# Sparse attention of the prompt: one sequence of heads across blocks, y transposes and output halves moved

## What is computed

```
for each block i of 128 queries, t = 128*i .. 128*i + 127:
    sc  = sum over 8 index heads of relu(iq . ik) * iw          (keys up to t)
    idx = top 256 of sc
    p   = softmax(q . k / 8 over idx), 8 heads, 2 key heads     y_dsa = p . v
out = concat(y_gla, y_dsa) @ w_out                              (1024 x 1024)
h   = layer_norm(alpha * x + out)
```

## Time and profile before

| | us |
|---|---|
| median of three executions | 3746.54 |
| lowest, highest | 3743.01, 3746.85 |
| the profiled execution, its time | 3748.45 |
| its span | 3746.8 |
| its mean granted clock of TensorE | 0.905 |

### The profile page before, as it was taken

One profiled execution on the slowest core, in us unless ns is written; L12 is line 12 of the kernel. 1 busy time (PEld: TensorE's weight loads), 2 busy tenths in 40 slices (PEclk: granted clock), 3 DMA queues, 4 the chain that ended last, 5 costly groups with the idle time before them and its releaser, 6 DMA issues. The chain is left out here.

```text
span 3746.8 us, 53513 instructions
## 1 busy us (share of the span) xinstructions
PE 3308.3 (88%) x20539; PEld 2829.9 (76%) x20539; DVE 1605.0 (43%) x2853; ACT 1089.8 (29%) x2145; POOL 340.2 (9%) x440
## 2 busy tenths in 40 slices
PE   8998884665798997999999997987997999999997
PEld 7797763343444555999999997983665999999997
DVE  2186661993676523111113564432454111113566
ACT  2223541323333233111113443212443111112443
POOL 1100102122111000000000002340000000000002
PEclk9998885786688778999999998996998999999999
DMA  4211014223000001111112111222001111112111
GB/s 130 57 35 30 24 35 118 68 67 127 29 17 17 14 15 40 45 45 45 45 39 98 39 49 48 49 69 86 32 25 43 45 45 41 43 45 94 40 56 49
DMA packets 238053, 190.85 MB, mean 51 GB/s; under 512 B 53762, under 2 KB 215956, under 8 KB 237844
## 3 DMA queue, kind: packets, MB, share of 16 engines
q1 hardware_dynamic: 230148, 170.73, 15.1%
q0 software_dynamic: 7728, 17.71, 1.5%
HBM read 158.73 MB, written 31.38 MB: 51 GB/s over the span
## 5 line engine op out<-in xcount | busy, mean ns | idle before, releaser
L1980 PE MATMUL ffn1u_ps<-h_hi,ffn1u_whi 128*128 128x384 f32 (+1 forms) x1056 | 348.0, 330 | 9.5 <-DVE h_lo L2042 9.5
L1980 PE MATMUL ffn0u_ps<-h_hi,ffn0u_whi 128*128 128x384 f32 (+1 forms) x1056 | 344.8, 327 | 8.8 <-DVE h_lo L2042 8.8
L1980 PE MATMUL ffn1u_ps<-h_lo,ffn1u_whi 128*128 128x384 f32 (+1 forms) x1056 | 347.9, 329 | 0.0
L1980 PE MATMUL ffn1u_ps<-h_hi,ffn1u_wlo 128*128 128x384 f32 (+1 forms) x1056 | 347.8, 329 | 0.0
L1980 PE MATMUL ffn0u_ps<-h_hi,ffn0u_wlo 128*128 128x384 f32 (+1 forms) x1056 | 344.9, 327 | 0.0
L1980 PE MATMUL ffn0u_ps<-h_lo,ffn0u_whi 128*128 128x384 f32 (+1 forms) x1056 | 344.8, 326 | 0.0
L197 PE MATMUL ine_ps<-ine_w_hi,ine_x_hi 128*128 128x256 f32 (+2 forms) x864 | 265.4, 307 | 5.1 <-DVE ine_w_lo L213 5.0
L197 PE MATMUL ine_ps<-ine_w_hi,ine_x_lo 128*128 128x256 f32 (+2 forms) x864 | 250.6, 290 | 0.0
L197 PE MATMUL ine_ps<-ine_w_lo,ine_x_hi 128*128 128x256 f32 (+2 forms) x864 | 250.2, 290 | 0.0
L1980 PEld LDWEIGHTS ffn1u_ps<-h_hi,ffn1u_whi 128*128 128x128 f32 x1056 | 198.9, 188 | 9.9 <-DVE ffn1u_wlo L2024 9.9
L1980 PEld LDWEIGHTS ffn0u_ps<-h_hi,ffn0u_whi 128*128 128x128 f32 x1056 | 198.7, 188 | 9.2 <-DVE ffn0u_wlo L2024 9.2
(11 more groups left out here) (464 smaller groups left out, 7344.7 us busy)
## 6 DMA issues: line engine op xcount, KB each, us to landing
ffn0u_raw<-in_ffn_w_gu_dram SPq DMA_DIRECT2D x44, 512.0 KB, 3.8
ffn1u_raw<-in_ffn_w_gu_dram SPq DMA_DIRECT2D x44, 512.0 KB, 3.8
ffn0d_w<-in_ffn_w_down_dram SPq DMA_DIRECT2D x88, 128.0 KB, 2.2
ffn1d_w<-in_ffn_w_down_dram SPq DMA_DIRECT2D x88, 128.0 KB, 2.2
smp_Kp<-in_cache_k_dram SPq DMA_DIRECT2D x128, 64.0 KB, 1.9
smp_Vp<-in_cache_v_dram POOLq DMA_DIRECT2D x96, 64.0 KB, 2.2
ine_w<-in_w_in_even_dram SPq DMA_DIRECT2D x5, 1024.0 KB
scratch_h<-ine_stage SPq DMA_DIRECT2D x20, 256.0 KB, 2.5
```

The source lines that it names most:

```text
L1980: last = nc.tensor.matmul(ps[:, t, k2, 0:n], wp[:, k2, k, :], hp[:, k, t0:t0 + n], start=(k == 0 and j == 0), stop=(k == KD - 1 and j == 2))
```

## The change

Four things are done, all in `dsa_out`:

1. The heads of all places form one sequence. Scores, row maximum and exponential of head 0 of place i + 1 are issued at the spot where those of a ninth head of place i would be: scores ahead of the transposes of head 7, the row maximum between the early and late rounds of head 7, the exponential after head 7's copies, ahead of `deviation`.
2. The y transposes of place i, with ACT's copies, move from the end of place i to place i + 1, behind the values of head 0 on PE and behind the exponential of head 1 and `scale` on ACT. `scale` of places 1 and later moves with them. The list of slots follows. The last place's stay at the end.
3. The query transposes of the next place come first in the list of passes, and the list no longer holds the output halves. The dots move up in it.
4. The output halves are added to the shares of heads 1 and 2 (the second and third head) behind what these hold already.

```diff
-        out = [("out", s, 0), ("out", s, 1)]
+        out, more = [("out", s, 0), ("out", s, 1)], []
         if s == 0:
-            out += [("iq", S0 + 1)] + dots(BLOCK[S0 + 1], range(2))
+            more = [("iq", S0 + 1)] + dots(BLOCK[S0 + 1], range(2))
...
-        if s + 1 < NT:
-            out.append(("q", s + 1))
-        return out
+        q = [("q", s + 1)] if s + 1 < NT else []
+        return q + more, out
...
-        u, r = passes(s), rounds(s)
+        (u, out), r = passes(s), rounds(s)
...
-        return [(u[n * per:(n + 1) * per], r[n * rper:(n + 1) * rper]) for n in range(NH)]
+        return [(u[n * per:(n + 1) * per] + out[n - 1:n][:n], r[n * rper:(n + 1) * rper]) for n in range(NH)]
...
+            if n == 0 and i >= 1:
+                slots += [("y", i - 1, 0), ("y", i - 1, 1)]
...
+                scores(0, 0)
                 for i in range(NT):
-                    T, share = tile(i), shares(i)
-                    scores(i, 0)
+                    share = shares(i)
                     for n in range(NH):
                         if n + 1 < NH:
                             scores(i, n + 1)
+                        elif i + 1 < NT:
+                            scores(i + 1, 0)
                         transpose_probs(i, n)
...
                         values(i, n)
-                    pe.wait_ge(y_done, i + 1)
-                    for hf in range(2):
...
+                        if n == 0 and i >= 1:
+                            y_transposes(i - 1)
+                y_transposes(NT - 1)
...
                         if n + 1 < NH:
                             exps(i, n + 1)
+                        elif i + 1 < NT:
+                            exps(i + 1, 0)
+                        if n == 0 and i >= 1:
+                            if i >= 2:
+                                scale(i - 1)
+                            copy_y(i - 1)
                     deviation(i)
...
                         if n + 1 < NH:
                             row_max(i, n + 1)
+                        elif i + 1 < NT:
+                            row_max(i + 1, 0)
```

More of the change, by code:

```diff
@@ L1032, in passes @@
             return [("index_keys", 0), ("index_keys", 1), ("iq", S0), ("keys", 0), ("keys", 1), ("q", 0)] + dots(BLOCK[S0], range(4))
[L1033 removed]
+        out, more = [("out", s, 0), ("out", s, 1)], []
         if s == 0:
[L1035 removed]
+            more = [("iq", S0 + 1)] + dots(BLOCK[S0 + 1], range(2))
         elif s == 1:
[L1037 removed]
+            more = dots(BLOCK[S0 + 1], range(2, 4))
         elif s + S0 < NT:
[L1039 to L1042 removed]
+            more = [("iq", s + S0)] + dots(BLOCK[s + S0], range(4))
+        q = [("q", s + 1)] if s + 1 < NT else []
+        return q + more, out
     def rounds(s):
@@ L1303, in _, with y_transposes @@
                         bank7(u)
+                def y_transposes(i):
+                    T = tile(i)
+                    pe.wait_ge(y_done, i + 1)
+                    for hf in range(2):
+                        slot_free(("y", i, hf))
+                        for k in range(4):
+                            c0 = (T_GR, T_DQ)[hf] + k * P
+                            last = nc.tensor.transpose(bank(("y", i, hf))[:, k * P:(k + 1) * P], T[:, c0:c0 + P], st.ident[:, :])
+                        last.then_inc(t_done, 1)
+                scores(0, 0)
                 for i in range(NT):
-                    T, share = tile(i), shares(i)
-                    scores(i, 0)
+                    share = shares(i)
                     for n in range(NH):
@@ L1403, in _, with copy_y @@
                     bank7(u)
+                def copy_y(i):
+                    for hf in range(2):
+                        act.wait_ge(t_done, number[("y", i, hf)] + 1)
+                        if hf == 0 and i >= 2:
+                            act.wait_ge(p7_done, pass_no[("out", i - 1, 1)] + 1)
+                        nc.scalar.copy(YT[:, i % 2, 4 * hf:4 * hf + 4, :],
+                                       bank(("y", i, hf)).rearrange("p (a t) -> p a t", a=4)).then_inc(t_read, 1)
+                exps(0, 0)
                 for i in range(NT):
                     share = shares(i)
-                    exps(i, 0)
                     for n in range(NH):
@@ L1414, in _ @@
                             exps(i, n + 1)
-                    deviation(i)
[L1416 to L1422, removed]
+                        elif i + 1 < NT:
[4 more added lines that the diff above has]
+                            copy_y(i - 1)
+                    deviation(i)
+                    if i == 0:
+                        scale(0)
+                copy_y(NT - 1)
+                scale(NT - 1)
                 copy_x(NT - 1)
```

17 lines of the change are left out of this document (7 added, 10 removed).

## The result

The changed kernel takes 3694.8 us (median of 4 executions, 3690.7 to 3714.8) against 3744.8 for the kernel before in the same comparison: a ratio of 0.9878, interval 0.9841 to 0.9914. A second comparison gave 0.9856, 0.9839 to 0.9872. The forecast was 3737, its range 3716 to 3753. One execution of the experiments, 6541.7 us at a granted clock of 0.57, was disturbed and is left out everywhere.

What follows compares the result with a forecast made beforehand. VectorE and what holds it up bound places 0 to 4, TensorE places 5 to 7. Terms -22.6 + 16.9 - 1.0 - 3.1 + 0.6 = -9.2 us took the median 3746.54 to 3737; range 3716 to 3753.

Steps and rivals of the forecast that it cites:

- (a): Boundaries into places 1 to 4: early head 0 removes VectorE's four first-row-maximum waits, 22.6 us gained at best.
- (b): Late y transposes remove TensorE's wait for the scaled output; three such waits go in places 5 to 7, 3.1 us.
- (c): Output halves at heads 1 and 2: VectorE's waits for them in places 0 to 4 go from 59.3 to 76.2, losing 16.9.
- the full-clock walk: Step-by-step count of place 2 with TensorE at full clock: VectorE waits 9.8 us for the halves, 11.7 before.
- rival 1: Half-clock stretches at three boundaries vanish with the idle time: about 28 us gained, 3718 us; chance 0.13.
- (d): Earlier dots and query transposes: shared-bank copy waits cost 0; small score waits inside heads of places 0 to 4 lose 1 us.
- (e): ScalarE's table switches stay two per boundary; waits for y's copy in places 6 and 7 cost 0.6 us, bounds 0 and 4.
- (f): SP's H ring reload and POOL's shift start later but are wanted later still: no effect, bound 1 us.
- Rival 3: Long products come a head later, the clock returning only during half 0: slower, 3762 us, or 3750 in milder form; chance 0.17.
- Rival 2: VectorE's longer waits for the halves use up the boundary gain: 3742 to 3750 us, 3746; chance 0.20.

Runs made afterwards that it cites:

- the kernel before with its fills: Kernel before plus useless products in the y waits ending places 0 to 3 and at heads 5, 6, 7 of every place: 3737.7 us.
- the one filled in places 0 to 4: Changed kernel plus six useless products ahead of the transposes of heads 5, 6 and 7 in places 0 to 4 only: 3690.2 us.
- changed kernel filled: Changed kernel plus six useless products ahead of the transposes of heads 5, 6 and 7 in every place: 3695.1 us.
- the filled boundary: Kernel before, order unchanged, plus 20 useless products in TensorE's wait for y at the ends of places 0 to 3: 3729.8 us.

## Why the prediction was wrong, step by step

**(a) Row maxima at the boundaries, -22.6: right.** All four waits are gone, though 4.35 us came back as waits of head 2 in places 2 and 4. The 22.6 also hold a part that is the old trace's half clock: in the kernel before with its fills the same four waits are 16.0. What I put down to the early head is won mostly by the late y, as the run without the early head shows.

**(b) The y wait, -3.1 in places 5 to 7: right.** One wait of 0.9 us is left, at the very end. TensorE's whole idle time there fell by less, from 14.6 to 13.3 us. Lengths times clock went from 128.6 to 125.9, 2.7 us. This measure is coarse: the changed kernel and the one filled in places 0 to 4 run the same instructions there and give 125.9 and 120.2. Counting time at half clock instead (67 to 26 us, worth half of 41) leaves 24.4 - 20.5 = 3.9 us to the order. All that these counts carry is that the order's own gain there is a few microseconds, as forecast.

**(c) The halves, +16.9: wrong, and the first of the two steps that failed.** The prediction said: "I take 16.9, because the earlier trace rows is the state in which each of these heads begins." The halves of places 2 and 3 in the changed kernel:

```profile
1036.39 0.69 DVE L1508 SCALAR_TENSOR_TENSOR dsa_X<-dsa_X,dsa_ps 128x512 f32<-128x512 f32 x1 [5.62 <-PE dsa_ps L1224]
...
1051.18 0.69 DVE L1508 SCALAR_TENSOR_TENSOR dsa_X<-dsa_X,dsa_ps 128x512 f32<-128x512 f32 x1 [5.59 <-PE dsa_ps L1224]
...
1116.30 0.69 DVE L1508 SCALAR_TENSOR_TENSOR dsa_X<-dsa_X,dsa_ps 128x512 f32<-128x512 f32 x1 [2.92 <-PE dsa_ps L1224]
...
1130.27 0.69 DVE L1508 SCALAR_TENSOR_TENSOR dsa_X<-dsa_X,dsa_ps 128x512 f32<-128x512 f32 x1 [5.94 <-PE dsa_ps L1224]
```

Place 2 waits 11.2 us where I took 16.7 and the full-clock walk gave 9.8; place 3 waits 8.9 where I took 19.0. All ten add up to 56.4, not 76.2, below the 60 at which the prediction called itself wrong (its other sign, a stage that changes by more than 25 us, was met too: 55.3). The term was mis-sized by 19.8 us: 3.8 in place 0, 5.5 in place 2, 10.1 in place 3, and 1 or less either way in the other two.

What failed is the extra that I put on for half clock. With the clock up (0.94, changed kernel filled) the ten waits add up to 51.1 us, and the walk at full clock had put them 8 below the 59.3, at 51.3. In place 3 I carried the half clock of the old trace into a schedule in which it isn't there: it is back at 1099.1, 0.6 us into the place and 17 before the first half is added. In place 2 the half clock was there as assumed, until 1024.0, 12.8 us into the place, but it cost less. The walk has half 0 end 25.7 us after the first row maximum at full clock and 7 later at half. It ended 28.7 us after it, so 3.0 later, and VectorE wanted it at 23.2, not 22.7. The clock at half through the first 10 us of place 0 cost less than assumed as well; that place I haven't taken apart.

**The clock in places 5 to 7: no term at all, the second failure.** The sum had 3.1 and 0.6 us of order there. The measured 24.4 us are mostly clock: 0.79 to 0.91, worth 20 to 22 by the two counts above. The runs don't show what raised it. The prediction's own view of the windows showed place 5 TensorE-bound at 0.73, so a change of clock acts on their full length, and it was priced nowhere, neither in the sum nor in rival 1, which counted only VectorE's waits in places 0 to 4. This is what put the result 21 us below the range's end.

**(d) 1 us of small score waits: mis-sized.** They went from 10.0 to 5.2 us, and 4.35 of the 5.2 are the new waits of head 2. The wait for the shared bank's copy is 2.0 us in three, in time that VectorE doesn't miss, as said.

**(e) Table switches: right where they were priced.** Head 1's transposes wait for y's copy 0.8 us in one in the late places, for which I had 0.6, and 2.7 us in two in places 0 to 4, where I had none; there TensorE doesn't set the time. The load starts 0.02 us after the read of the accumulator ends (1094.76, 1094.78), and the square root at 1096.08, again 0.02 us after the load: no drain, so the further 4 us that the Trainium skill (ScalarE: Activation LUTs, What ACT_TABLE_LOAD costs) would add didn't come in this order either.

**(f) SP and POOL: nothing**, as said.

**The rivals.** Rival 1 is the nearest, but only part of it took place. Its figure for places 0 to 4 (22.6 + 8 + 1 = 31.6) stands beside 30.7 measured, though its parts came out otherwise (halves 2.9, small waits 4.8). Of its three stretches one shrank and two grew, and the stage's mean clock is 0.85, where it asked for 0.90. I gave it 0.13 because a stretch began ahead of the wait and because short heads lose the clock by themselves. Both are true and neither answers the question, which is when the clock comes back. With a 4.59 us wait in the middle the stretch into place 3 lasted 23.8 us with TensorE busy 78% of it; with none and 95% busy it lasted 10.2. The Trainium skill (TensorE: Matmul & The Clock Gate, HAM oscillation) says that a wait between bursts that throttles the array makes each next burst start slow; the filled boundary agrees as far as it goes (0.50 to 1.00 behind it, 18.9 us), though the stretch that is gone had begun ahead of the wait. And a wait is not all of it: the changed kernel keeps about 152 us at half clock without a wait for y at the boundaries, and the 61 us piece with the halves together is 94% busy. Rival 3 had the clock come back with the long products of half 0; in places 2 and 3 of the changed kernel it came back 5 and 10 us before they began (at 1029.1 and 1109.0). Rival 2's own sum, 4 to 8 us above the forecast, gives 3741 to 3745, not the 3742 to 3750 it states. Rivals 2 and 3 are the time that the kernels with one part missing take (3747, 3759), not that of the whole.

**What stays open.** Why the clock comes back after 10 us at one boundary and 27 at another is not settled: 9.67 of 10.20 us busy in one, 26.27 of 27.20 in the other. Nor is why the executions of one kernel fall into groups 20 us apart (the early head without the late y: 3722, 3729, 3747, 3770), nor what sets the clock of places 5 to 7, some 20 us of the 50: the early head there is worth 9.4 us of it, the fills far ahead, in places 0 to 4, cost 8.2. Whether idle time or the kind of work decides is open as well. A run that removes the waits without adding products or moving other work, or one that adds the products only where there is no wait in places 0 to 3, would tell more.

## What to carry to other kernels

Where the granted clock is below 1, a change of order is priced twice: once by its waits, and once by the clock that the work behind them will then have; don't carry the old trace's clock into the new schedule as a given, but make both sums and let the range hold both. Do the second sum first for the stretches that TensorE bounds, since it acts there on their whole length: 0.79 to 0.91 on 163 us is about 20 us, and all idle TensorE in them was 14.6. And test parts of such a change together as well as alone: here spreading the halves alone cost 11 us, the rest with both halves at one head gained nothing, and the whole gained 50.

## What the runs showed of the hardware

- Useless products in a wait are not only harmless, they can pay: 4.48 to 7.2 us of them at each of four boundaries took 18.9 us off. The same kind inside heads that don't wait cost 7.9 us in the kernel before.
- The half clock lasts through busy time: 61 us at 0.50 with TensorE 94% busy, 27.2 us with it 97% busy.
- The clock of a stretch depends on what ran long before: the same instructions in places 5 to 7 took 138.4 us at 0.91 or 146.6 us at 0.82, with fills that ended before them in the second case.
- Orders differ in how widely their executions scatter: 3742 to 3752 before, 3730 to 3771 with the halves together, 3690.7 to 3695.4 and once 3714.8 in the changed kernel's eight.
